# Softmax scaling by ScalarE in place and TensorE transposes, instead of a product with a diagonal from VectorE, in the attention of a two-block hybrid model

## The reference, cut to what matters

```python
def context_attention(q, k, v):      # q, k, v: (batch, head, token, 64)
    ...                              # softmax(q k^T / 8) v
def neighbourhood_attention(q, k, v, k_ctx, v_ctx, rpb):
    ...                              # softmax over window keys (with bias rpb) and context keys
```

## Time and profile before

| what | us |
|---|---|
| time, median of 3 runs (lowest, highest) | 3039.07 (3038.74, 3042.73) |
| span of the profiled execution, first to last instruction | 3030.3 |
| median less that span (what lies around it) | 8.8 |
| PE busy | 2855.5 (94%) |
| DVE busy | 1568.4 (52%) |
| POOL busy | 1266.1 (42%) |
| ACT busy | 1068.2 (35%) |

### The profile page before, as it was taken

How to read it: one execution, slowest core, us unless ns; L and a number is a source line. 1 busy time by engine, 2 the same in 40 slices (tenths; PEclk the granted TensorE clock), 3 DMA queues, 4 the chain that set the end, 5 groups by cost and what they waited for, 6 DMA issues and landing times.

```text
span 3030.3 us, 41702 instructions
## 1 busy us (share of the span) xinstructions
PE 2855.5 (94%) x15864; PEld 2327.7 (77%) x15864; DVE 1568.4 (52%) x2050; ACT 1068.2 (35%) x1579; POOL 1266.1 (42%) x696
## 2 busy tenths in 40 slices
PE   6999987999999998999989999999999998899997
PEld 6974745878888887777767888888787777688886
DVE  6875684451224463387765423423347876652525
ACT  4435233332333232335433322313343453342433
POOL 3452102443544370587623322222348773344443
PEclk9999998999999999999999999999999999999998
DMA  5327595322332333422221211221233212223332
GB/s 177 94 89 251 164 299 185 101 96 86 111 91 85 115 112 125 132 77 77 68 65 59 80 63 62 63 63 62 77 91 97 74 60 70 83 90 93 94 97 70
DMA packets 115578, 306.91 MB, mean 101 GB/s; under 512 B 36128, under 2 KB 44448, under 8 KB 114784
## 3 DMA queue, kind: packets, MB, share of 16 engines
q1 hardware_dynamic: 86000, 284.22, 29.7%
q10 hardware_dynamic: 28864, 18.76, 2.2%
q0 software_dynamic: 560, 1.84, 0.2%
HBM read 294.95 MB, written 7.45 MB: 100 GB/s over the span
## 4 chain that ended last, share of the span: by engine, by line
PE 76%; DVE 10%; DVEq 4%; ACT 3%; DMA 2%; issue 2%; POOL 1%; ACTq 1%; SPq 0%; POOLq 0%
PE ps L298 36%; PE ps L328 17%; PE ps L319 6%; PE ps L1893 3%; DVE co L2186 2%; PE ps L2299 2%; DVEq L2187 2%; PE ps L1951 2%; PE ps L1897 1%; DMA mt<-ka 1%; PE ps L1898 1%; PE ps L1901 1%; POOL wlo L259 1%; PE ps L715 1%; DVE mv L2378 1%
## 5 line engine op out<-in xcount | busy, mean ns | idle before, releaser
L259 POOL TENSOR_TENSOR wlo<-wraw,whi 128x1024 fp32r<-128x1024 f32 x373 | 923.3, 2485 | 1446.0 <-ACT whi L251 1444.5
L251 ACT ACTIVATE whi<-wraw 128x1024 fp32r<-128x1024 f32 x373 | 391.9, 1054 | 485.5 <-PE ps L328 157.8
L298 PE MATMUL ps<-xhi,whi 128*128 128x512 f32 (+1 forms) x1328 | 469.8, 370 | 1.7 <-issue 1.7
L298 PE MATMUL ps<-xlo,whi 128*128 128x512 f32 (+1 forms) x1328 | 470.6, 371 | 0.0
L298 PE MATMUL ps<-xhi,wlo 128*128 128x512 f32 (+1 forms) x1328 | 334.0, 371 | 0.0
L298 PEld LDWEIGHTS ps<-xhi,whi 128*128 128x128 f32 x1328 | 240.5, 188 | 48.1 <-issue 2.7
L298 PEld LDWEIGHTS ps<-xlo,whi 128*128 128x128 f32 x1328 | 240.5, 188 | 44.5
L298 PEld LDWEIGHTS ps<-xhi,wlo 128*128 128x128 f32 x1328 | 232.3, 188 | 44.7
L2186 DVE SCALAR_TENSOR_TENSOR co<-ub,vec,co 128x512 f32<-128x512 f32 (+1 forms) x216 | 226.9, 1090 | 6.1 <-issue 1.3
L2285 POOL TENSOR_TENSOR co<-co,ct 128x512 f32<-128x512 f32 (+1 forms) x144 | 164.8, 1144 | 20.5
L1076 DVE SCALAR_TENSOR_TENSOR res<-ps,mod,res 128x512 f32 (+1 forms) x64 | 47.7, 749 | 222.0 <-PE ps L319 132.2
(11 more groups left out here) (395 smaller groups left out, 5695.8 us busy)
## 6 DMA issues: line engine op xcount, KB each, us to landing
wraw<-stream SPq DMA_DIRECT2D x425, 512.0 KB, 3.5
wada<-w_ada SPq DMA_DIRECT2D x56, 512.0 KB, 7.6
wraw<-w_ada SPq DMA_DIRECT2D x40, 512.0 KB, 3.9
biasb<-attn_bias ACTq DMA_DIRECT2D x32, 256.0 KB, 3.8
xin<-x0T SPq DMA_DIRECT2D x4, 528.0 KB, 6.3
s_u<-uk ACTq DMA_DIRECT2D x8, 264.0 KB, 3.8
res<-x0T ACTq DMA_DIRECT2D x1, 2048.0 KB, 9.0
s_y<-yk ACTq DMA_DIRECT2D x64, 32.0 KB, 4.9
```

Of the source, the lines that this page charges most:

```text
L251: act.activation(whi[:, s], wraw[:, s], ACT.Copy).then_inc(hi_done[s], 1)
L259: pool.tensor_tensor(wlo[:, s], wraw[:, s], whi[:, s].bitcast(F32), ALU.subtract).then_inc(lo_done[s], 1)
L298: last = pe.matmul(ps[:, bank, 0:b - a], w[:, s, kt], x[:, kt, c0 + a:c0 + b], start=start, stop=stop)
```

## The change

The diagonal matrices are gone. VectorE still takes the reciprocals and signals them with a new step `rec`. ScalarE multiplies both heads' exponentials in `pex` by the reciprocals, in place, as two activations with the function Copy and a scale read from `sm`. TensorE transposes the blocks of `pex` with `transpose`.

```diff
@@ in build
-    dg0 = at("dg0", [P, P], O_C + 4 * CONST["tri"])
-    dg1 = at("dg1", [P, P], O_C + 4 * CONST["keep"] + 2048)
-    dg = (dg0[:, :], dg1[:, :])
@@ in turn_pe
-                last = pe.matmul(ps[:, 6 + h, b * P:(b + 1) * P], pex[:, h, b * P:(b + 1) * P], dg[h], start=True, stop=True)
+                last = pe.transpose(ps[:, 6 + h, b * P:(b + 1) * P], pex[:, h, b * P:(b + 1) * P], ident)
@@ new
+    def scale_act(act, p, n):
+        c = 2 * (n % 2)
+        act.wait_ge(p.a_rec.sem, p.a_rec.past("rec", n))
+        for h in range(2):
+            x = pex[:, h, 0:p.W]
+            ins = act.activation(x, x, ACT.Copy, scale=sm[:, 2, c + h:c + h + 1])
+        ins.then_inc(p.a_sc.sem, 1)
@@ in mix_act
         for n in range(p.N + 2):
+            if 0 < n <= p.N:
+                scale_act(act, p, n - 1)
             for g in late:
                 evac_act(act, p, g)
@@ in scale_dve
         dve.wait_ge(p.a_exp.sem, p.a_exp.past("exp", n))
-        dve.reciprocal(sm[:, 2, c:c + 2], sm[:, 1, c:c + 2])
-        dve.drain()
-        for h in range(2):
-            ins = dve.tensor_scalar(dg[h], ident, sm[:, 2, c + h:c + h + 1], None, ALU.mult)
-        ins.then_inc(p.a_sc.sem, 1)
+        dve.reciprocal(sm[:, 2, c:c + 2], sm[:, 1, c:c + 2]).then_inc(p.a_rec.sem, 1)
```

More of the change, by code:

```diff
@@ L1782, in __init__ @@
             self.c_g = s("conv_taps", "conv", passes=self.taps - 1)
-            self.a_s, self.a_max, self.a_exp, self.a_sc, self.a_turn, self.a_pt, self.a_pv = (
-                s(f"attn_{k}", k, passes=self.N) for k in ("scores", "max", "exp", "scaled", "turned", "copied", "values"))
+            self.a_s, self.a_max, self.a_exp, self.a_rec, self.a_sc, self.a_turn, self.a_pt, self.a_pv = (
+                s(f"attn_{k}", k, passes=self.N) for k in ("scores", "max", "exp", "rec", "scaled", "turned", "copied", "values"))
             self.o_a, self.o_v = s("aout_hi", "hi", passes=4), s("aout_lo", "lo", passes=4 * two)
```

## The result

The change takes 3021.86 us (median of 4 runs, 3015.81 to 3027.71) where the kernel before takes 3040.90 (4 runs, 3038.74 to 3056.98): ratio 0.9931, 95% interval 0.9912 to 0.9950. It is faster, by 19 us where 33 were forecast, and it lies above the range of 2999 to 3017. Run again (6 runs) it took 3023.41 us, ratio 0.9928 (0.9900 to 0.9955).

A forecast was written before the change was run, and what follows sets the result against it. PE was taken to bound steps 0 to 9 and c0, DVE's ring steps 10 to 15. Gains of 13.8 us in each of two latent passes and 5.2 in c0, 32.8 in all, gave 3006 us, range 2999 to 3017.

The forecast's parts named there:

- The turn: PE's turning of pex blocks in each attention step: 1.10 us shorter in latent passes, 0.65 in c0.
- The tails from values 15 to the layer norm unchanged within 1 us: Behind each latent loop, PE's and DVE's remaining work moves forward equally, its length unchanged within 1 us.
- PE, not DVE, paces: Steps 0 to 9 of a latent pass run on PE, 10.3 us each in steps 5 to 9.
- DVE, 0.5 us a step for the diagonals: Steps 10 to 14 of a latent pass: dropping the diagonals shortens DVE's ring, 5 x 0.5 = 2.5 us.
- The next tap inherits most of the wait: On DVE, the tap behind the reciprocal takes over most of the diagonals' hold-up, so 0.5 us is counted, not 1.0.
- ACT, 1.3 us for the pair without a table load: ACT's two scaling activations take 1.3 us, cost nothing in steps 0 to 9, and 0.8 us at each latent loop's end.
- Rival 1: PE alone sets the time, DVE's hold-ups go with the diagonals: 40.4 us of gain, 2999 us; chance 0.12.
- Rival 2: In steps 10 to 15 DVE's or ACT's ring gives nothing back: 25.2 us of gain, 3014 us; chance 0.15.
- Rival 3: In steps 10 to 15 waits lower TensorE's clock, losing 1 us in up to 12 steps: 3018 us; chance 0.07.
- Rivals 4 and 5: Slower through ACT's queue, 3076 or 3051 us, chance 0.05; transposes as costly as the product, about 3035, chance 0.04.
- the 8.8 us: Added to the profiled span of 3030.3 us, so that the kernel before stands at its median of 3039.1.

The follow-up runs named there:

- the transposes alone: Kernel before with its products of the pex blocks made transposes, diagonals still written and waited for, rows unscaled: 3037.26 us, ratio 0.9991.
- two of the experiments: Kernel before with only the transposes put in, diagonals still written: 3037.26 us; the change with VectorE also writing the unused diagonals: 3031.89 us.
- the other half: The change with TensorE's transpose replaced by a product with the identity, keeping the DVE and ACT parts: 3033.55 us, ratio 0.9979.

## Why the forecast was wrong

The mechanism held: a transpose has half the records of the product, the pair on ACT hides, and the gain is PE's in the main. Three terms failed: the turn's size, the loops of steps 0 to 9 as PE's alone, and the tails taken as unchanged.

- **The turn, 1.10 and 0.65 us: mis-sized.** 0.96 and 0.50. I took four transposes from a chain row of another line (0.44) and doubled it for eight; other chain rows of that line in the same trace have 0.63 for four. Measured, four take 0.58 and eight 1.02: 0.11 for each one more, and 0.14 that the row of L1914 didn't show. Half of the old turn's own row, 1.98 / 2 = 0.99, would have been nearer. The sum counts 11 turns in a latent pass: 22 x 0.14 + 8 x 0.15 = 4.3 us too much.
- **"The tails from values 15 to the layer norm unchanged within 1 us": failed.** They grew by 2.3 and 1.3 us. PE and DVE met at the layer norm with 0.68 us between them, and I moved both by the same amount. But POOL's work stays as long as it was, so in a shorter loop more of it is left over DVE's tail: POOL's last tap ends 17.1 us behind the loop before and 18.6 us after, and DVE's 26 tap instructions, 33.65 us from the first to the last before, took 37.06. The other profiles agree: where POOL ends 17.1 us behind the loop the 26 take 33.1 to 33.7 us, at 17.8 us 34.3, from 18.1 us up 36.6 to 37.5, and without POOL's taps 28.0 to 28.5. The wait became 1.98.
- **"PE, not DVE, paces" steps 0 to 9: half right.** I read steps 5 to 9 of `l1` and let them stand for ten. In `l1` PE waited 3.2 us for k posts before (two times) and 5.7 us after (three times). With the turn's size put right the forecast has 12.3 us for a latent loop; the change got 11.8 and 9.2, and 11.4 and 10.9 in its second profile. DVE's ring was close behind PE's, which the transposes alone lay bare: 7 us for 35 us of PE's work, the fall of the clock behind `c0` left out. The chain shows which ring is longest, not how near the next one is.
- **DVE, 0.5 us a step for the diagonals: right in size, partly by luck.** Put back, they cost 2.6 and 3.3 us a loop, for 2.5 forecast, but only 2.0 of the 5.9 us are waits. The rest is slower work of PE behind them, which the term didn't hold. "The next tap inherits most of the wait" is what the busy times show (26.7 before, 27.0 after). The Trainium skill (SBUF — State Buffer, on the shared port pair) has VectorE and GpSimd lock one port pair for a whole instruction, for copies in a two-port mode and for forms with two SBUF inputs, and never for tensor_reduce. The trace agrees for three forms: beside POOL's taps the copy of 64x128 takes 1058 ns for 220 and the tap instruction 1184 for 832, and the maximum stays at 1225 for 1224. What I missed is that a hold-up that only moves still lengthens the ring when it lands on a post in steps 0 to 9, where there was no room.
- **ACT, 1.3 us for the pair without a table load: right** (1.33). From reciprocal to turn at the last step 1.57 were forecast and 2469.14 - 2467.55 = 1.59 measured. In steps 0 to 9 no turn waits for it.
- **Rival 1** (PE alone, 40 us) has no support: even without POOL's taps it is 31. **Rival 2** (the rings give nothing back in steps 10 to 15; 3014) is off by 8 us and misplaces the loss, which is spread over early posts, late taps and tails. **Rival 3** (clock; 3018) comes nearest in time, but by luck: it had 12 us in steps 10 to 15, and in both loops together the change lost 0.5 to 2.2 us more to slower work than the kernel before. In steps 10 to 15 of `l1` the granted clock was 1.00 in spite of PE's waits, as the first window below shows; in `l0` it did fall, around the turn of step 13, as the second shows, and in the second profile around the turn of step 14 of `l1` instead. It also cost 4.6 us behind `c0` in two of the experiments, with no wait longer than in the others. **Rivals 4 and 5** didn't occur.

Windows of the change, steps 10 to 15 of `l1` and 3 us around the turn of step 13 of `l0`:

```profile
2413.00:2475.00 62.00, 57.59 (x363) 44.32 (x362) 46.44 (x44) 50.19 (x70) 49.76 (x33) 1.00 0.19 60
1446.50:1449.50 3.00, 2.12 (x12) 1.79 (x14) 2.93 (x5) 2.97 (x5) 0.09 (x1) 0.68 0.02 5
```

One more figure was misread, though it did no harm to the difference: the 8.8 us "around" the span. In every later execution the time is the span and 1.8 us; the median run was simply another execution than the profiled one.

The sum again, with what was measured: 32.8 less 4.3 for the turn's size is 28.5. The loops have 25.0 (26.3 in the second profile), so 3.5 (2.2) were kept in them; the tails took 3.6 (2.4) and the stretches between and behind 1.0 (1.9). That leaves 20.4 and 22.0, where the table has 20.7 and 22.3; the 0.3 is rounding. How the 3.5 divide between the early posts, the taps of steps 10 to 15 and the clock differs between the two profiles, and isn't settled further.

## What to carry to other kernels

Before counting a shorter instruction as gain, find the second-longest ring in each step, not only the longest: here the shorter turn alone gave 7 of its 35 us, the other half 7, and both together 21 to 22. Where two engines hold each other up, leave the amount of work and move it to where the victim waits anyway; that was worth 14 to 16 us from `c0` on, not much less than the change itself. Add up a loop as work and as waiting before naming the cause of a difference: here a wait also made the work behind it slower. Judge a change in one stage by that stage's rows when the stages that it doesn't touch move by 18 us from one execution to the next.

## What was not expected of the hardware

- The stretch ahead of `c0`, the same code in every kernel, lasted from 1034.6 to 1052.3 us. The windows from 200 to 300 us show it, the kernel before and then the change:

```profile
200.00:300.00 100.00, 89.15 (x653) 52.22 (x652) 53.74 (x75) 52.67 (x151) 36.24 (x19) 0.93 0.57 200
```

```profile
200.00:300.00 100.00, 90.63 (x577) 53.63 (x575) 48.66 (x67) 49.94 (x147) 36.03 (x20) 0.86 0.49 168
```

  At a granted clock of 0.86 PE did 577 instructions where it did 653 at 0.93. Whether the clock is the whole of the difference, and what makes it differ between executions, wasn't found.
- A copy of 64x128 on DVE takes 0.22 us with POOL quiet and 1.06 us on average beside POOL's taps, as the rows by line show, and a tap instruction 0.83 and 1.18: of these two the smaller one bears by far the larger share.
